# Recurrent-gate weights taken through the shared ring of weight slots, and their fp32 products replaced by three split products

## The reference

```python
xb = xf.reshape(B, S, N_RNN_BLOCKS, RNN_BLOCK)                 # 8 blocks of 256 features
r = sigmoid(einsum('bsni,nij->bsnj', xb, w_a) + b_a)
i = sigmoid(einsum('bsni,nij->bsnj', xb, w_x) + b_x)
log_a = -LRU_C * r * softplus(-lam)
a = exp(log_a); mult = sqrt(-expm1(2.0 * log_a))
b = mult * (i * xf)                                            # h = scan(a, b) over the tokens
y_rnn = h * gelu(yr)                                           # yr: another 2048 columns of x @ w_in
```

## Time and profile before

| what | value |
|---|---|
| median of 3 runs | 2237.97 us (2237.29 to 2238.43) |
| the profiled execution | 2237.42 us, its span 2235.7 us |
| PE busy | 2226.1 us |
| DVE, ACT, POOL busy | 1576.1, 1223.2, 273.8 us |
| granted TensorE clock | 1.0 of full throughout |

### The profile page before, as it was taken

The page is one execution under the profiler, slowest core; times in us unless marked ns, Lnnn a source line. Parts: engine busy times, 40 slices in busy tenths (PEclk is TensorE's granted clock), DMA queues, the critical chain, the costliest instruction groups (busy, mean ns, idle before and its releaser), DMA issues.

```text
span 2235.7 us, 32769 instructions
## 1 busy us (share of the span) xinstructions
PE 2226.1 (100%) x11630; PEld 1872.6 (84%) x11630; DVE 1576.1 (70%) x2081; ACT 1223.2 (55%) x1924; POOL 273.8 (12%) x317
## 2 busy tenths in 40 slices
PE   9999999999999999999999999999999999999999
PEld 7888999888888888888888888889977788888887
DVE  6666657664664778857857856966999967766774
ACT  6666667544444456555655656556444446554443
POOL 2232220000000102111212121220000000100000
PEclk9999999999999999999999999999999999999999
DMA  7555454666656866666666666665566655555665
GB/s 245 152 170 151 149 181 142 194 192 194 192 189 197 255 197 199 217 206 189 220 206 193 213 210 203 194 220 185 180 188 203 195 181 166 169 161 178 198 201 166
DMA packets 215349, 427.09 MB, mean 191 GB/s; under 512 B 14096, under 2 KB 14384, under 8 KB 214960
## 3 DMA queue, kind: packets, MB, share of 16 engines
q1 hardware_dynamic: 206960, 398.57, 57.0%
q0 software_dynamic: 8048, 26.62, 3.8%
q10 hardware_dynamic: 208, 0.07, 0.0%
HBM read 414.71 MB, written 10.49 MB: 190 GB/s over the span
## 4 chain that ended last, share of the span: by engine, by line
PE 91%; DVE 4%; ACT 3%; issue 1%; DMA 1%; POOL 0%; SPq 0%; ACTq 0%; POOLq 0%; DVEq 0%
PE acc L2043 25%; PE acc L2045 25%; PE acc L2044 25%; PE acc L2035 4%; PE acc L2037 3%; PE acc L2038 3%; DVE w_lo L1209 1%; PE sides L2263 1%; ACT w_hi L677 1%; PE tps L2273 1%; PE sides L2136 1%; DMA raw<-in_w_in_dram 1%; PE tps L2154 1%; PE tps L2147 0%; DVE stg L1233 0%
## 5 line engine op out<-in xcount | busy, mean ns | idle before, releaser
L1209 DVE TENSOR_TENSOR w_lo<-raw,w_hi 128x1024 fp32r<-128x1024 f32 x752 | 928.0, 1243 | 585.4 <-ACT w_hi L677 579.8
L677 ACT ACTIVATE w_hi<-raw 128x1024 fp32r<-128x1024 f32 x752 | 789.8, 1057 | 728.3 <-PE acc L2045 595.2
L2043 PE MATMUL acc<-w_hi,h_hi 128*128 128x512 f32 x1424 | 563.2, 396 | 1.2 <-DVE h_lo L1284 0.9
L2045 PE MATMUL acc<-w_hi,h_lo 128*128 128x512 f32 x1424 | 554.9, 390 | 0.0
L2044 PE MATMUL acc<-w_lo,h_hi 128*128 128x512 f32 x1424 | 554.5, 389 | 0.0
L2043 PEld LDWEIGHTS acc<-w_hi,h_hi 128*128 128x128 f32 x1424 | 267.3, 188 | 67.5 <-issue 11.4
L2045 PEld LDWEIGHTS acc<-w_hi,h_lo 128*128 128x128 f32 x1424 | 267.3, 188 | 56.7
L2044 PEld LDWEIGHTS acc<-w_lo,h_hi 128*128 128x128 f32 x1424 | 267.5, 188 | 53.0
L2044 PE MATMUL acc<-w_lo,slab_dg_r 128*128 128x512 f32 x756 | 294.1, 389 | 0.0
L2043 PE MATMUL acc<-w_hi,slab_dg_r 128*128 128x512 f32 x756 | 294.1, 389 | 0.0
L2045 PE MATMUL acc<-w_hi,slab_dg_r 128*128 128x512 f32 x756 | 294.1, 389 | 0.0
(11 more groups left out here) (406 smaller groups left out, 2354.2 us busy)
## 6 DMA issues: line engine op xcount, KB each, us to landing
raw<-in_w_in_dram SPq DMA_DIRECT2D x328, 512.0 KB, 4.0
raw<-in_w_mlp_up_dram SPq DMA_DIRECT2D x128, 512.0 KB, 4.2
raw<-in_w_mlp_down_dram SPq DMA_DIRECT2D x128, 512.0 KB, 4.2
raw<-in_w_out_dram SPq DMA_DIRECT2D x64, 512.0 KB, 4.4
raw<-in_w_rnn_proj_dram SPq DMA_DIRECT2D x32, 512.0 KB, 3.8
raw<-in_w_attn_proj_dram SPq DMA_DIRECT2D x32, 512.0 KB, 3.7
trig_scratch<-tmp POOLq DMA_DIRECT2D x32, 256.0 KB, 4.8
raw<-in_w_proj_ssm_dram SPq DMA_DIRECT2D x16, 512.0 KB, 3.8
```

The costliest lines, as they stand in the source:

```text
L677: nc.scalar.activation(w_hi[:, j % RING], raw[:, j % RING], ACT.Copy).then_inc(hi_ready, 1)
L1209: V.tensor_tensor(w_lo[:, j % RING], raw[:, j % RING], w_hi[:, j % RING].bitcast(F32), ALU.subtract)\
L2043: T.matmul(o, hi[:, k, c], wh, start=first, stop=False)
L2045: ins = T.matmul(o, lo[:, k, c], wh, start=False, stop=last)
```

## The change

The gate weights no longer have buffers of their own. Each group gets two slots of the ring, one for each of its two blocks, right behind slot 0 of the unit that holds it. Such a unit now has 10 slots, and all later slot numbers move (`first_slot`). SP loads such a slot with two transfers of 256 KB; ACT and DVE split it as any other. POOL's `load_rg` goes; in its place `split_conv` splits the convolved input in two parts (`xc_hi`, `xc_lo`), one copy and one subtraction of 1024 elements a partition for each group. PE runs `head_gates` with 24 matmuls of 256 columns for each of the two slots, instead of `rg`. The hooks of the recurrence are hung at later steps. SP's loops over the `yr` and mix units are written out.

```diff
+        def first_slot(u):
+            return u * S + 2 * min(max(u - U_YR - 1, 0), NH)
+        def gate_slot(c, b=0):
+            return first_slot(U_YR + 1 + c) + 1 + b
-        rgw = [[slab_g[:, 0:4, :], slab_g[:, 4:8, :]], [slab_e[:, 12:16, :], slab_i[:, 12:16, :]]]
+        xc_hi, xc_lo = [slab_gr[:, 0:4, :], slab_er[:, 12:16, :]], [slab_gr[:, 4:8, :], slab_ir[:, 12:16, :]]
...
+            def load_gates(c, b):
+                g = gate_slot(c, b)
+                sp.wait_ge(lo_ready, g - LEAD)
+                for name, at, landed in (("w_rg_x", 1, gate_x_landed), ("w_rg_a", 0, raw_landed[g % RING])):
+                    sp.dma_start(raw[:, g % RING, :, at * SEQ:(at + 1) * SEQ],
+                                 a[name][0][2 * c + b].rearrange("(t p) n -> p t n", p=P)).then_inc(landed, 16)
...
-                    def load_rg(c):
...
+                    def split_conv(c):
+                        pool.wait_ge(conv_ready, c + 2 if c != 1 else NH + 1)
+                        if c >= 2:
+                            pool.wait_ge(pe_used, gate_slot(c - 2, 1) + 1)
+                        xc = slab_d[:, c * QPC:(c + 1) * QPC, :]
+                        chain.link(pool.tensor_copy(xc_hi[c % 2], xc))
+                        pool.tensor_tensor(xc_lo[c % 2], xc, xc_hi[c % 2].bitcast(F32), ALU.subtract).then_inc(xc_parts, 1)
...
                         if c == 0:
-                            load_rg(0)
+                            split_conv(0)
+                    for c in range(1, NH):
+                        split_conv(c)
...
             def gates(c):
-                act.wait_ge(rg_done, c + 1)
+                act.wait_ge(pe_used, gate_slot(c, 1) + 1)
...
-                places = {0: [lambda: gelu(c)], 1: [lambda: gates(c)], 2: [lambda: decays(c)], 4: [lambda: root(c)]}
+                places = {0: [lambda: gelu(c)], 3: [lambda: gates(c)], 4: [lambda: decays(c)], 6: [lambda: root(c)]}
                 if c < NH - 1:
-                    places[7] = [lambda: y_high(c)]
+                    places[9] = [lambda: y_high(c)]
...
-                return {3: [lambda: decay(c)], 5: [lambda: states(c)], 6: [lambda: y_product(c)], 7: [lambda: y_low(c)]}
+                return {5: [lambda: decay(c)], 7: [lambda: states(c)], 8: [lambda: y_product(c)], 9: [lambda: y_low(c)]}
...
+            def head_gates(c, b):
+                g = gate_slot(c, b)
+                if b == 0:
+                    pe.wait_ge(xc_parts, c + 1)
...
+                pe.wait_ge(lo_ready, g + 1)
+                for e, bank in enumerate((tps[:, b * NC:(b + 1) * NC], side[b][:, :])):
+                    for m in range(2):
+                        o = bank[:, m * SEQ:(m + 1) * SEQ]
+                        at = slice(e * SEQ + m * P, e * SEQ + (m + 1) * P)
+                        for k in range(2):
+                            wh, wl = w_hi[:, g % RING, k, at], w_lo[:, g % RING, k, at]
+                            hi, lo = xc_hi[c % 2][:, 2 * b + k, :], xc_lo[c % 2][:, 2 * b + k, :]
+                            T.matmul(o, wh, hi, start=k == 0, stop=False)
+                            T.matmul(o, wh, lo, start=False, stop=False)
+                            ins = T.matmul(o, wl, hi, start=False, stop=k == 1)
+                ins.then_inc(pe_used, 1)
```

More of the change, by code:

```diff
@@ L398, in unit, with unit_with_gates @@
                     load(weights, col, k0 + 2 * s, g0 + s, s)
+            def unit_with_gates(weights, col, u, c):
+                g = first_slot(u)
+                for s in range(S):
+                    load(weights, col, 2 * s, g, g)
+                    g += 1
+                    if s == 0:
+                        for b in range(2):
+                            load_gates(c, b)
+                            g += 1
             def past(i, stride, const):
@@ L1014, in mlp_units @@
                         hooks[3] = [lambda c=n - 5: e_squares(c)]
-                    steps(f, 8 * S, u * S, hooks, start=5 if n == 0 and f is None else 0)
+                    steps(f, 8 * S, first_slot(u), hooks, start=5 if n == 0 and f is None else 0)
                     if n < 4:
-                        unit_over(f, 8 * S, u * S)
+                        unit_over(f, 8 * S, first_slot(u))
                         act.wait_ge(blocks_turned, lin(f, 4, V_MLP + 4 * b + n))
@@ L1717, in mlp_units @@
                         return
-                    steps(f, 8 * S, u * S, hooks, start=5 if b == 0 and n == 0 else 0)
+                    steps(f, 8 * S, first_slot(u), hooks, start=5 if b == 0 and n == 0 else 0)
                     at = slice((n - 4) * NC, (n - 3) * NC)
@@ L1997, in unit @@
                 for s in range(k_tiles // 2):
+                    slot = g0 + s + (2 if gates is not None and s else 0)
                     for f in before.get(s, []):
@@ L2019, in unit @@
                             for e in range(2):
-                                wh, wl = w_hi[:, s % RING, e, :], w_lo[:, s % RING, e, :]
+                                wh, wl = w_hi[:, slot % RING, e, :], w_lo[:, slot % RING, e, :]
                                 T.matmul(o, hi[:, 2 * s + e, c], wh, start=False, stop=False)
@@ L2049, in unit @@
                             f()
+                    if gates is not None and s == 0:
+                        for b in range(2):
+                            head_gates(gates, b)
+            def head_gates(c, b):
+                g = gate_slot(c, b)
+                if b == 0:
+                    pe.wait_ge(xc_parts, c + 1)
+                    if c:
+                        pe.wait_ge(w_ready, c)
+                    else:
+                        pe.wait_ge(att_out, 4 * NH)
+                pe.wait_ge(lo_ready, g + 1)
[10 more added lines that the diff above has]
+                ins.then_inc(pe_used, 1)
             def turn(i, stride, t_index, blocks=QPC):
```

133 lines of the change are left out of this document (58 added, 75 removed).

## The result

The changed kernel takes 2242.68 us (median of 14 runs, 2242.41 to 2242.91), the one before 2237.44 (14 runs beside them, 2236.29 to 2238.43): a ratio of 1.0023, 95% interval 1.0016 to 1.003. It is 5.2 us slower. The profiled span is 2240.7 us, 5.0 over that of before, and the granted TensorE clock is 1.0 in both.

What follows compares the result with a forecast made beforehand. PE was taken to bound the stage, busy for all its 29.94 us. -4.56 (PE) + 10.5 (ring) + 0.8 (POOL) = +6.7 us on 2237.4 gave 2244.1, 2244.7 as median; stated 2244.5, range 2239.5 to 2248.5.

Steps and rivals of the forecast that it cites:

- PE saves 4.56 us: Gates on PE: 2 x 24 matmuls at 0.12 pitch, 5.76 us, replace a 6.90 us fp32 block; 1.14 us a group.
- The ring loses 10.5 us: Three-slot ring: splits late for PE without the fp32 gates' rest; 9.9 us waits, 1.0 restarts, less 0.4 from before.
- the nine waits: PE waiting for late splits at gate, `yr` and first mix unit slots, 311 to 408 us; 9.9 us in sum, longest 1.7.
- GpSimd adds 0.8 us at the queries' turn: Near 120 us: group 0's copy and subtraction hold DVE's rotation by the port lock, so PE waits 0.8 us.
- The gates' transfers are free: Loads of gate slots: 3.7 to 6.0 us needed against 9.7 us of cover, so no cost.
- the 9.7 us of cover: Slot 11: time from when it can be loaded (T = 15) until ACT wants it (24.7).
- Slower by over 0.2%: Verdict for the whole kernel: time over 2242.4 us, given chance 0.74.
- The rival on the other side: DVE's and ACT's splits are ready when wanted, PE's saving stands alone: 2233.4 us; chance 0.08, half under 2233.5.

Runs made afterwards that it cites:

- spread-out version: Changed kernel with ACT's and DVE's recurrence side work at other steps, `y_high` and `y_low` carried into the next unit: 2231.88 us, ratio 0.9975 to the kernel before.
- the last placing: Changed kernel with side work spread out and GpSimd's first split later, but ACT's gates at step 3 instead of 2: 2234.85 us, ratio 0.9988 to the kernel before.

## Why the prediction was right

It said 2244.5 us (2239.5 to 2248.5) and slower; it is 2242.7, and each term can be compared, in the profiled executions.

- **PE saves 4.56 us.** Right. A gate slot's matmuls are 0.12 apart, and the first such unit, 29.14 us, is 10 x 2.88 = 28.8 and its one wait of 0.22 with a restart of 0.10.
- **The ring loses 10.5 us.** Right: eight waits of 9.48 us, 0.88 of restarts, less the 0.36 of before, 10.0. Forecast for the places of the nine waits: 0.3, 1.3, 0.2, 1.3, 1.3, 1.6, 1.4, 0.8, 1.7; measured 0.22, 1.35, none, 1.34, 1.36, 1.48, 1.48, 0.60, 1.65. The missing one (0.2, slot 15) left only its restart. The stage from 285 to 407 us so costs 5.5 us net (the last slot of the first mix unit begins at 406.95 instead of 401.04, and the stage began 0.42 later), where 5.9 were forecast.
- **GpSimd adds 0.8 us at the queries' turn.** The mechanism was right, the size was double: 0.4. I had DVE's rotation (118.28) held to the subtraction's end at 120.1; GpSimd's copy got the port at 116.2, sooner than I had it, and the subtraction ended at 119.86. The copy's 1.05 us is 1.04 alone (at 294.34 us).
- **The gates' transfers are free.** Right in the time; loading the slots otherwise changes nothing. But the 9.7 us of cover are those of a unit's first gate slot. The second one of group 3 was issued from 370.58 and ACT was free for it at 374.67, 4.1 us later; it began at 376.19. That this cost nothing is due to DVE's being later still, which the forecast did not work out.
- **Not in the forecast:** 0.8 us given back at 865 to 885 us. I had carried the stage's loss to the end unchanged. With it, 5.5 + 0.4 - 0.8 = 5.1 us, where the spans differ by 5.0 and the medians by 5.2.

The three terms that were off, 0.4, 0.4 and 0.8 us, had the same sign: they take the forecast of +6.7 us to +5.1. The other part of the 1.8 us between 2244.5 and 2242.7 is not the change's. The forecast stood on a median of three runs, 2237.97; fourteen runs give 2237.44, 0.5 us less. The sum had been rounded down by 0.2.

"Slower by over 0.2%" came out narrowly: the ratio is 1.0023, and its interval begins at 1.0016. With 0.8 us more given back somewhere it would have been "same", so in that word there is some luck; in the mechanism and in the places of eight of the nine waits there is not.

The rival on the other side, that the queues keep up, did not come true for this kernel. It needed `states` 1.3 us sooner. In the spread-out version, with the hooks of both engines placed anew, the queues do keep up, and PE's saving stands alone (2231.9 us). That says how near the arrangement was, and nothing of the chance of 0.08 for the one that was forecast.

## What to carry to other kernels

Faster matmuls pay only if their operands are ready at the new pace: a slow block that takes no operand from a ring is also the ring's rest, and who removes it must count what caught up in it. In a ring three slots deep and with in-order queues, lay out for each producer the stretches of other work between two of its slots. What decided here is such a stretch, together with how late the producer already is when it comes, and not the producer's busy share (DVE was busy for 73% of the three units above with the waits, and for 80% of 285 to 400 us in the spread-out version, 91.9 of 115 us, without any). Put the transfers into that layout too: in the last placing an operand that had not landed held all that stood behind it. So after such a change place the side work anew, split what is longer than a slot, and carry over what nobody is waiting for, before judging it: the same arithmetic went from 5.2 us slower to 5.8 us faster.

## What the runs showed of the hardware

- DVE and GpSimd hold each other where DVE reads two operands of SBUF, and in these rows not where one of the two is the accumulator: beside one subtraction of GpSimd's (117.39 to 119.86) the rotation's steps that read the accumulator took their 0.68 us, the step with two SBUF operands 1.32 instead of 0.43. It works both ways: GpSimd's copy of 1.04 us took 1.92 behind a split (285.17), its phase operations 1.59 instead of 0.60 (862.05).
- The same store of 256 KB by GpSimd's queue, near 855 us, was waited for 4.8 to 4.9 us in two profiles of one program and 2.9 to 3.2 us in one profile each of its twelve near relatives (the later stores of that loop 3.5 to 6.6 us in all of them). A difference below 1 us far from an edit can come of such a shift, and not of what the edit was meant to do.
- Sixteen more loads of 256 KB beside the mix units, one every 3.4 to 6.1 us, cost nothing that shows (2242.75 us against 2242.68).
